# Second layer's score products over 64 rows in place of zero-padded copies of k

## What is computed

```
qk = silu(causal_depthwise_conv(u @ w_in[qk part]))     # q: 8 heads x 64, k: 8 heads x 64
s   = (q . k) * 64**-0.5 * exp(b_t - b_s + i_s - m_t)    # s <= t, gates i, f give b and m
num = s @ v ;  den = sum(s)
h   = num / max(|den|, exp(-m_t))
out = (sigmoid(o) * rms_norm(h)) @ w_o
```

## Time and profile before

| | us |
|---|---|
| median of 3 runs | 1305.01 |
| lowest and highest | 1304.06 and 1309.29 |
| span of the profiled execution | 1303.4 |
| TensorE busy in it | 1227.1 (94%) |
| VectorE busy | 686.6 (53%) |
| ScalarE busy | 454.7 (35%) |
| GpSimd busy | 292.2 (22%) |
| DMA, mean | 80 GB/s |

### The profile page before, as it was taken

One profiled execution on the slowest core, in us unless ns is written; L12 is line 12 of the kernel. 1 busy time (PEld: TensorE's weight loads), 2 busy tenths in 40 slices (PEclk: granted clock), 3 DMA queues, 4 the chain that ended last, 5 costly groups with the idle time before them and its releaser, 6 DMA issues.

```text
span 1303.4 us, 15832 instructions
## 1 busy us (share of the span) xinstructions
PE 1227.1 (94%) x5829; PEld 1012.0 (78%) x5829; DVE 686.6 (53%) x955; ACT 454.7 (35%) x725; POOL 292.2 (22%) x255
## 2 busy tenths in 40 slices
PE   6888999899999999999997999889999999999997
PEld 4667777678888888888876997666888888888885
DVE  5867888734534434334479434795443343343432
ACT  4336666543212212222342324763322221221242
POOL 4222222222201102002134103562220020110211
PEclk8999999999999999999999999899999999999998
DMA  4201011222232332322222322011323223233211
GB/s 151 67 22 27 23 26 32 87 77 85 97 108 87 106 96 88 105 89 97 89 75 65 125 86 73 25 49 34 100 94 100 95 97 99 94 98 96 97 65 64
DMA packets 113887, 104.00 MB, mean 80 GB/s; under 512 B 20934, under 2 KB 112164, under 8 KB 113836
## 3 DMA queue, kind: packets, MB, share of 16 engines
q1 hardware_dynamic: 113344, 102.98, 25.2%
q10 hardware_dynamic: 492, 0.31, 0.1%
HBM read 101.17 MB, written 2.11 MB: 79 GB/s over the span
## 4 chain that ended last, share of the span: by engine, by line
PE 76%; DVE 11%; issue 6%; ACT 3%; POOL 3%; DMA 0%; ACTq 0%; DVEq 0%; POOLq 0%
PE ps L1473 23%; PE ps L1475 23%; PE ps L1474 23%; DVE nmax L1113 2%; POOL xl L570 1%; DVE xl L972 1%; DVE yc L1290 1%; DVE qtmp L1105 1%; DVE diag L987 1%; POOL wlo L513 1%; ACT whi L638 1%; ACT prob L714 1%; ACT uh L728 1%; DVE rinv L1118 1%; DVE yc L1287 1%
## 5 line engine op out<-in xcount | busy, mean ns | idle before, releaser
L1473 PE MATMUL ps<-xl,whi 128*128 128x512 f32 (+1 forms) x688 | 270.7, 394 | 5.3 <-DVE krot L1052 3.2
L638 ACT CAST whi<-raw 128x2048 fp32r<-128x2048 f32 (+4 forms) x150 | 184.7, 1259 | 247.9 <-PE ps L1475 239.5
L1475 PE MATMUL ps<-xh,wlo 128*128 128x512 f32 (+1 forms) x688 | 268.6, 390 | 0.0
L1474 PE MATMUL ps<-xh,whi 128*128 128x512 f32 (+1 forms) x688 | 268.6, 390 | 0.0
L967 DVE TENSOR_TENSOR wlo<-raw,whi 128x2048 fp32r<-128x2048 f32 (+2 forms) x86 | 187.5, 2184 | 151.9 <-ACT whi L638 151.9
L1473 PE MATMUL ps<-ul,whi 128*128 128x512 f32 x608 | 237.3, 390 | 1.2 <-POOL wlo L513 1.2
L1475 PE MATMUL ps<-uh,wlo 128*128 128x512 f32 x608 | 236.7, 389 | 0.0
L1474 PE MATMUL ps<-uh,whi 128*128 128x512 f32 x608 | 236.6, 389 | 0.0
L543 POOL TENSOR_TENSOR ul<-sq,uh 128x512 fp32r<-128x512 f32 x64 | 83.6, 1308 | 521.2 <-ACT uh L817 521.2
L1195 DVE TENSOR_TENSOR h<-ps,h 128x512 f32<-128x512 f32 x80 | 55.0, 689 | 197.4 <-PE ps L1475 192.5
L1473 PEld LDWEIGHTS ps<-xl,whi 128*128 128x128 f32 (+1 forms) x688 | 129.0, 188 | 35.1 <-issue 4.9
(11 more groups left out here) (234 smaller groups left out, 1653.1 us busy)
## 6 DMA issues: line engine op xcount, KB each, us to landing
raw<-in_mlp_w SPq DMA_DIRECT2D x64, 1024.0 KB, 5.2
raw<-in_mlstm_w_in SPq DMA_DIRECT2D x12, 1024.0 KB, 5.4
raw<-in_mla_w_o SPq DMA_DIRECT2D x4, 1024.0 KB, 5.0
raw<-in_mlstm_w_o SPq DMA_DIRECT2D x4, 1024.0 KB, 5.4
raw<-in_mla_w_in SPq DMA_DIRECT2D x3, 1024.0 KB, 5.6
raw<-in_mla_w_uq SPq DMA_DIRECT2D x16, 192.0 KB, 2.5
x_tok<-in_x SPq DMA_DIRECT2D x4, 512.0 KB, 5.9
mb<-m_rows SPq DMA_DIRECT2D x8, 256.0 KB, 3.2
```

What stands on the lines that cost most here:

```text
L638: last = sc.copy(hi, src)
L1473: mm(o, ah, bl, start=first, stop=False)
L1474: mm(o, ah, bh, start=False, stop=False)
L1475: ins = mm(o, al, bh, start=False, stop=last)
```

## The change

The score product takes both operands with the head's own 64 partitions only, `rows = slice(64 * e, 64 * e + 64)`: the weights are read from the k tile in `uh`/`ul`, the moving operand from the q tile. The buffers `mkh`/`mkl`, their copies, their memsets and their semaphores are gone. TensorE waits once for `y_lo` (all low parts of q and k) where it waited for `mk_zero`. TensorE's loop over pairs becomes a Python loop, so that its two iterations are written out with fixed addresses; the other engines keep theirs.

```diff
-        mkh = C("mkh", [P, 2, S], F32R)
-        mkl = C("mkl", [P, 2, S], F32R)
@@ GpSimd
-            pool.wait_ge(y_lo, 8)
-            for e in range(2):
-                rows = slice(64 * (1 - e), 64 * (1 - e) + 64)
-                g.memset(mkh[rows, e, :].bitcast(F32), 0.0)
-                own.link(g.memset(mkl[rows, e, :].bitcast(F32), 0.0))
-            g.nop().then_inc(mk_zero, 1)
@@ VectorE
-            def k_copy(i, lead):
-                e, pair = lead % 2, i + lead // 2
-                rows = slice(64 * e, 64 * e + 64)
-                for dst, src in ((mkh, uh), (mkl, ul)):
-                    last = v.tensor_copy(dst[rows, e, :], src[rows, ds(pair + 4, 1), :]
-                                         .rearrange("p a s -> p (a s)").bitcast(F32))
-                last.then_inc(mk_ready, 1)
@@ VectorE, before the first heads
                 if j == 2:
-                    dve.wait_ge(y_lo, 8)
                     for e in range(2):
-                        k_copy(0, e)
                         masked(0, e)
@@ VectorE, head_step
                 if not last and not first:
-                    k_copy(i, lead + 1)
                     masked(i, lead + 1)
@@ TensorE, st_product
-                    if j == 0:
-                        pe.wait_ge(mk_ready, i * 2 + (lead + 1))
                     o = ps[:, B_ST + z % 2, 0:LEN[j]]
-                    part = slice(P * j, P * j + P)
-                    qt = [x[:, ds(pair, 1), P * j:S].rearrange("p a s -> p (a s)") for x in (uh, ul)]
-                    product(o, [((mkh[:, e, part], mkl[:, e, part]), qt)]).then_inc(st_mm, 1)
+                    part, rows = slice(P * j, P * j + P), slice(64 * e, 64 * e + 64)
+                    kt = [x[rows, pair + 4, part] for x in (uh, ul)]
+                    qt = [x[rows, pair, P * j:S] for x in (uh, ul)]
+                    product(o, [(kt, qt)]).then_inc(st_mm, 1)
@@ TensorE
-            pe.wait_ge(mk_zero, 1)
+            pe.wait_ge(y_lo, 8)
             st_product(0, 0, (0, 1))
...
-            with pe.Fori(1, MPAIRS - 1) as i:
+            for i in range(1, MPAIRS - 1):
                 head_step(i, 1)
                 head_step(i, 2)
```

More of the change, by code:

```diff
@@ L284, in trunk @@
         g_t, gcol_ready = sem("g_t"), sem("gcol_ready")
-        mk_zero, den_mm, den_read = sem("mk_zero"), sem("den_mm"), sem("den_read")
-        md_ready, mk_ready, mv_hi, mv_lo = sem("md_ready"), sem("mk_ready"), sem("mv_hi"), sem("mv_lo")
+        den_mm, den_read = sem("den_mm"), sem("den_read")
+        md_ready, mv_hi, mv_lo = sem("md_ready"), sem("mv_hi"), sem("mv_lo")
         st_mm, w_exp, sw_mul, sw_hi, sw_lo = sem("st_mm"), sem("w_exp"), sem("sw_mul"), sem("sw_hi"), sem("sw_lo")
```

## The result

| | us | ratio to before, 95% interval |
|---|---|---|
| before | 1305.01 (1304.06 to 1309.29) | 1 |
| after | 1309.69 (1308.70 to 1310.34) | 1.003, 1.0017 to 1.0042 |
| forecast | 1301.1, range 1297.0 to 1308.0 | 0.997 |

The changed kernel is 0.3% slower. That is within the 0.5% that the prediction calls no change, but the time lies 8.6 us above the forecast, outside the range, and on the other side of the kernel before. The profiled span went from 1303.4 to 1307.9 us, its mean granted clock from 0.981 to 0.970.

A forecast was written before the change was run, and what follows sets the result against it. TensorE bounds nearly everywhere, but VectorE sets the pace in the steady head steps. Copies −4.3, switches between projection tiles +0.35, the rest 0, sum −3.9 us: 1305.0 − 3.9 = 1301.1 us, range 1297.0 to 1308.0.

The forecast's parts named there:

- The copies: Five steady head steps: removing VectorE's k copies gains 0.90 us in three and 0.78 in two, 4.3 us in all.
- The wait that was to appear before `rb`: Steady head steps: VectorE idles briefly for TensorE's answer to `diag`, with 1.2 us from `diag` to `rb`.
- The loop, the memsets, the waits for `y_lo`: TensorE's written-out pair loop, GpSimd's dropped memsets and TensorE's new wait for low parts: each worth 0.
- The tail: After the heads: the last `diag` stays held (5.03 us) behind GpSimd, TensorE then bounds, and the gain is carried.
- A 64-row matmul costs as much as a 128-row one: Score products on TensorE: 96 matmuls with half the rows take unchanged time.
- The price of a switch: TensorE, changing between 128-row and 64-row matmuls: 0.09 us each, bounded by 0 and 0.35; six a head, 0.5 us.
- The prediction's own point at which TensorE would become the pace: Steady steps: from 0.18 us a switch TensorE decides the pace; from about 0.33 the saving is gone; chance 0.15.
- between the projection tiles: Four switches at 796.8 and 803.5 us, where TensorE never waits, are not hidden and cost 0.35 us.
- a full stop: Upper end for one switch: a matmul ends before the next weight load begins, 0.35 us more.
- The first heads: First head steps (817 to 823 us): four switches cost 0.35 us, the third head's missing copies give 0.3, together 0.
- The rival: Head stage: half-filled score products leave the clock at the low level, 12.5 us a step, 1323 us; chance 0.04.

The follow-up runs named there:

- e3: The changed kernel with all 128 rows of the q and k tiles contracted in place, mixing two heads' scores; 1300.23 us, ratio 0.9959.
- e4: The kernel before with the k copies made by DMA on SyncE's queue instead of VectorE, 128-row products, loop kept; 1299.38 us, ratio 0.9956.
- e13: The changed kernel contracting 96 rows for every head, which mixes heads; 1299.74 us, ratio 0.9952.
- e1: The kernel before with only TensorE's pair loop written out; 1305.29 us, ratio 0.9995.
- e8: e4 with the second MLP's two middle quarters contracting only partitions 0 to 63; one execution, span 1299.9 us against e4's 1297.6.
- e10: e4 with the second MLP's two middle quarters alternating 128-row and 64-row products, 256 switches; one execution, span 1351.2 us against e4's 1297.6.
- e5: e4, loop written out, with a one-row, one-column transpose behind each of a head's three score groups; 1303.79 us, ratio 0.9981.
- e14: e4, loop written out, with a one-row, one-column transpose ahead of each of a head's three score groups; 1301.32 us, ratio 0.9970.
- e11: e4 with one-row transposes both ahead of and behind each score group, six a head; 1308.03 us, ratio 1.0016.
- e12: e4, loop written out, with the eight one-column matmuls of a head's sums issued twice; 1302.58 us, ratio 0.9981.
- e17: The changed kernel with three full 128x512 matmuls added ahead of each head's one-column sums, results unused; 1310.02 us, ratio 1.0024.

## Why the prediction was wrong

**The copies: right.** e3, e4 and e13 have no VectorE copies and the full clock in the steady steps. Their five steady steps take 44.22 us against 48.41 before, 4.2 less; the term was 4.3. The wait that was to appear before `rb` appeared (0.18 us). With them the kernel would have come to 1299.4 to 1300.2, near the forecast.

**The loop, the memsets, the waits for `y_lo`: right,** each worth nothing (e1; e4 with the loop and e13 without it have the same 44.22 us). The tail too: 410.48 us against 410.68, the last `diag` still held for 5.02 us behind GpSimd.

**A 64-row matmul costs as much as a 128-row one: right** (pitch 0.23 us in e8, 0.24 between two of its kind above).

**The price of a switch: mis-sized.** "I take 0.09 us a switch" is half of it; the rows show 0.19 to 0.20 and e10 0.20 to 0.21. The error was in the reading of the earlier trace rows: I measured the one gap at each end, and the next gap carries the other half. The row behind those of the earlier trace rows shows it, 0.22 us after 740.98 where the pitch is 0.12:

```profile
741.20 0.28 PE L1474 MATMUL ps<-whi,xh 128*128 128x256 f32 x1
```

The prediction's own point at which TensorE would become the pace was 0.18 us a switch, so by its formula the steps were on the edge. They were not over it: of the six switches one was there before (block 2 follows the one-row transposes in both kernels), and e5, with six added switches a head at full clock, leaves TensorE 0.67 us of waiting, though its steps are 0.21 us longer than e4's. Where nothing hides the switches they do cost: between the projection tiles the stretch from the matmul ahead of the first score product to the last tile matmul grew by 0.59 us in place of 0.35 (12.98 to 13.57). The Trainium skill had spoken against the change here (TensorEngine Tiling (Array Packing), Key Properties: a change of tiling mode drains TensorE, a change of tile does not). The trace agrees that there is a price, and puts it at 0.19 us, between my 0.09 and the 0.35 of a full stop.

**The first heads: 0 was wrong.** From the last tile matmul to the first steady `diag` it is 21.47 us where it was 19.99, +1.48. Three to four switches are 0.7 of that by the price above. The granted clock of the stretch is 0.68 where it was 0.83, so it was at the lower level for 13.7 us instead of 6.8; that this made the rest is argued, not shown, as TensorE also waits there.

**The failed step is the clock.** The rival was named, with the mechanism as it came (TensorE at the 1.2 GHz level through numerator, sums and `norm_spread`, TensorE becoming the pace), and put aside with "Nothing in the rows says that it depends on rows; chance 0.04". In the steady steps the change and e4 differ by 50.76 − 44.22 = 6.5 us, with 23 of the change's 50.76 us at the lower level. e5, with one added switch a step more than the change but the clock at 1.00, has only 1.05 us of that, so some 5.5 us go with the clock. At most half of 23.3 is lost work, so at full clock TensorE would need at least 50.76 − 11.7 = 39.1 us, 7.8 us a step; from the other side, e4's (44.22 − 7.1) / 5 = 7.4 us (7.1 us are its waits for `diag`) and five switches of 0.19 make 8.4. Both are under the pace of 8.85 us. So without the fall of the clock TensorE would not have become the pace, and by e5 the forecast would have stood but for some 1 us in the steps.

The rival's size (1323) was too high, since it had the lower level in every step from the numerator to `norm_spread`, 12.5 us a step. In the trace a short stretch (the 3.5 us of 839.70 to 843.20) and a long one (the 6.5 us of 850.10 to 856.60) take turns, and the paces with them: 9.33, 9.64, 11.11, 9.49 and 11.19 us.

What the prediction could have seen: the earlier trace rows show that in this very stage, with full rows, the clock had already fallen to 0.57 once, with no wait of TensorE longer than 1.5 us in that step. The same trace has two more such stretches in the head steps, 0.50 in 814.5 to 821.3 us and 0.60 in 882.8 to 886.9 us, which the prediction did not look at. A stage that is near such a fall is not to be given 0.04 when an edit adds breaks to its stream.

**What lowers the clock is narrowed, not settled.** Shown not to be enough by itself: empty rows (e13), 64-row products in a dense stream (e8), 256 switches in a dense stream (e10), six and four added switches a step between full products (e5, e14; their whole-run clock is e4's within 0.001 in all executions). Shown to be enough in this stage: ten added switches with full rows (e11), which are six more one-column matmuls too. That longer one-column sums are enough (e12) is not shown. The runs agree with one reading: this stage, with its one-column sums, is close to a fall of the clock in the kernel before (23 of its 90 executions were as long as the changed kernel), and each further break or one-column matmul brings more of it to the lower level. That reading is argued, not shown. Two things stay open in it: why e5 has 1.00 and the change 0.77 with one break fewer, and why e17's filler kept the clock in two executions of seven only. e5's products have all rows and the change's half; e8 and e13 don't exclude that this matters, as rows and breaks may be needed at once.

## What to carry to other kernels

Before shrinking the contraction of a few matmuls between full ones, count the switches of row shape: each costs about 0.2 us on TensorE here, in two gaps, and a height of 96 needs none. Look at more executions than the profiled one: a kernel some of whose executions are longer at a lower whole-run clock has a stage that is close to the fall. Where a stage mixes matmuls of one column with full ones and its granted clock has dipped in the profile, price a fall of the clock to the lower level over the whole stage, since it turns an engine with 1.5 us of spare time a step into the pace. And when only another engine's copies are in the way, move the copies (here to DMA, 1299.4 us, 0.44% under before) rather than change the shape of the matmuls that read them.

## What had not been expected of the hardware

- A switch between 128 and 64 rows stretches two gaps, 0.32 and 0.33 us for 0.23, and the first matmul behind it has 0.49 to 0.50 us in its row for 0.39. One-row transposes count as such a switch, 96 rows don't.
- The granted clock went down where TensorE became busier: 50.76 busy of 50.76 us at 0.77, against 37.08 of 44.22 at 1.00 in e4. Busy time in the rows does not tell whether the clock will hold.
- SBUF-to-SBUF copies of 128 KB by DMA take 3.5 us (`mkh`) and 3.9 us (`mkl`) from issue to landing in e4 (medians of eight), far inside a head's 8.85 us, at no cost to VectorE.
